# Attention in rounds: two query blocks share a slot between TensorE's main matmuls, and a slot runs transposes, scores, values

## What is computed

```python
# first block: window of 128 keys, per query block the block before and its own
scores = jnp.einsum("bnqhgd,bnkhd->bnhgqk", q, kw) * ATTN_SCALE
scores = jnp.where(mask, scores, -jnp.inf)
probs = softmax(concatenate([scores, sink]))[..., :-1]
out = jnp.einsum("bnhgqk,bnkhd->bnqhgd", probs, vw)
...
# second block, each of two layers: chunk and the eight chunks before it
scores = jnp.einsum("bnqhd,bnkhd->bnhqk", qc, kb) * (dh ** -0.5)
scores = jnp.where(valid, scores + bias, NEG_INF)
out = jnp.einsum("bnhqk,bnkhd->bnqhd", softmax(scores), vb)
```

## Time and profile before

| | |
|---|---|
| median of 3 runs | 1231.44 us (1231.25 to 1232.39) |
| the profiled execution | 1231.82 us |
| its span | 1229.7 us |
| PE busy | 1220.1 us, 99% |
| DVE, ACT, POOL busy | 711.3 us (58%), 535.8 us (44%), 87.2 us (7%) |
| chain that ended last | 95% PE |

### The profile page before, as it was taken

The page is one execution under the profiler, slowest core; times in us unless marked ns, Lnnn a source line. Parts: engine busy times, 40 slices in busy tenths (PEclk is TensorE's granted clock), DMA queues, the critical chain, the costliest instruction groups (busy, mean ns, idle before and its releaser), DMA issues.

```text
span 1229.7 us, 16394 instructions
## 1 busy us (share of the span) xinstructions
PE 1220.1 (99%) x5966; PEld 985.6 (80%) x5966; DVE 711.3 (58%) x1352; ACT 535.8 (44%) x956; POOL 87.2 (7%) x79
## 2 busy tenths in 40 slices
PE   9999999999999999999999999999999999999998
PEld 7888777888888888888888887778888887778886
DVE  5555765464577776775652546654555236564654
ACT  4522553444444344342242414454654325454653
POOL 3000000001100000000010100033002000033000
PEclk9999999999999999999999999999999999999999
DMA  6333222322333223333223521222223431122221
GB/s 210 106 101 103 70 69 69 102 87 87 102 103 102 80 91 102 102 103 102 85 96 103 205 82 58 68 69 69 69 69 111 164 100 55 52 69 69 69 86 69
DMA packets 98203, 114.06 MB, mean 93 GB/s; under 512 B 3801, under 2 KB 82875, under 8 KB 98011
## 3 DMA queue, kind: packets, MB, share of 16 engines
q1 hardware_dynamic: 95755, 107.69, 26.6%
q10 hardware_dynamic: 2384, 5.51, 1.3%
HBM read 111.05 MB, written 2.14 MB: 92 GB/s over the span
## 4 chain that ended last, share of the span: by engine, by line
PE 95%; DVE 1%; ACT 1%; issue 1%; DMA 1%; POOL 0%; SPq 0%; DVEq 0%; ACTq 0%; POOLq 0%
PE main L574 22%; PE main L576 22%; PE main L575 22%; PE aux L664 3%; PE aux L574 3%; PE aux L576 3%; PE aux L575 3%; PE aux L643 3%; PE main L883 2%; PE main L885 2%; PE main L884 2%; PE aux L655 2%; PE main L958 1%; PE main L957 1%; PE main L956 1%
## 5 line engine op out<-in xcount | busy, mean ns | idle before, releaser
L574 PE MATMUL main<-x_hi,w_hi 128*128 128x512 f32 x984 | 393.6, 400 | 0.2 <-DVE w_lo L1459 0.2
L576 PE MATMUL main<-x_hi,w_lo 128*128 128x512 f32 x984 | 383.8, 390 | 0.0
L575 PE MATMUL main<-x_lo,w_hi 128*128 128x512 f32 x984 | 383.7, 390 | 0.0
L1378 DVE TENSOR_TENSOR w_lo<-raw,w_hi 128x1024 fp32r<-128x1024 f32 x192 | 237.9, 1240 | 250.7 <-ACT w_hi L998 246.6
L998 ACT ACTIVATE w_hi<-raw 128x1024 fp32r<-128x1024 f32 x192 | 202.3, 1055 | 260.0 <-PE main L576 156.0
L576 PEld LDWEIGHTS main<-x_hi,w_lo 128*128 128x128 f32 x984 | 184.7, 188 | 40.1
L574 PEld LDWEIGHTS main<-x_hi,w_hi 128*128 128x128 f32 x984 | 184.9, 188 | 38.2 <-issue 2.1
L575 PEld LDWEIGHTS main<-x_lo,w_hi 128*128 128x128 f32 x984 | 185.2, 188 | 35.2
L1036 ACT ACTIVATE soft_pair<-soft_pair,neg_peak 128x256 f32<-128x256 f32 (+3 forms) x64 | 33.6, 526 | 50.4 <-DVE neg_peak L1431 50.4
L1415 DVE TENSOR_TENSOR up_in<-main,factor 128x512 f32<-128x512 f32 x44 | 30.4, 690 | 37.9 <-PE main L576 34.9
L883 PE MATMUL main<-w_hi,x_hi 128*128 128x512 f32 x128 | 50.5, 394 | 0.0
(11 more groups left out here) (264 smaller groups left out, 1837.3 us busy)
## 6 DMA issues: line engine op xcount, KB each, us to landing
raw<-in_w_in_dram SPq DMA_DIRECT2D x98, 512.0 KB, 4.4
raw<-in_w_up_dram SPq DMA_DIRECT2D x44, 512.0 KB, 3.9
raw<-in_w_out_dram SPq DMA_DIRECT2D x24, 512.0 KB, 4.0
raw<-in_w_down_dram SPq DMA_DIRECT2D x22, 512.0 KB, 4.2
rel<-band_rows ACTq DMA_DIRECT2D x2, 2048.0 KB, 9.5
x_rows<-in_x_dram SPq DMA_DIRECT2D x4, 512.0 KB, 8.0
raw<-in_w_attn_branch_dram SPq DMA_DIRECT2D x4, 512.0 KB, 3.4
raw<-in_w_conv_branch_dram SPq DMA_DIRECT2D x4, 512.0 KB, 4.4
```

Of the source, the lines that this page charges most:

```text
L574: pe.matmul(bank, hi, right_hi[j], start=first and j == 0, stop=False)
L575: pe.matmul(bank, hi, right_lo[j], start=False, stop=False)
L576: done = pe.matmul(bank, lo, right_hi[j], start=False, stop=last and j == len(rows) - 1)
L1378: dve.tensor_tensor(w_lo[:, u % 4, :, :], raw_unit(u), w_hi[:, u % 4, :, :].bitcast(F32), ALU.subtract).then_inc(lo_ready, 1)
```

## The change

The two attentions' steps are grouped into rounds, each with up to four key blocks per head (eight rounds in the first block, ten in each layer of the second). A slot now works on rounds: transposes of round r - 2, scores of round r, values of round r - 3, in this order. In the first block there is one slot per unit, after its fourth k-step (11 slots, units 20 to 30); in the second a slot comes every six k-steps, from k-step 92 of the layer (unit 11, after its fourth) on (13 slots, up to unit 20). DVE normalises round r - 1 ahead of softening round r. ACT and DVE place a slot ahead of the unit's own work as before. The transposes use the banks `aux[2]` and `main[3]` in the first block too, so that its units 20 to 30 share three main banks. The tiles for probabilities hold 512 columns per half, two in turn.

```diff
+ROUNDS1 = [[(t, 2 * j), (t, 2 * j + 1)] for t in range(4) for j in range(2)]
+ROUNDS2 = [steps for t in (0, 2) for steps in
+           ([(t, 0), (t, 2)], [(t, 3)], [(t + 1, 0), (t + 1, 2)], [(t, 1), (t + 1, 1)], [(t + 1, 3)])]
+ATT2_SLOTS = [92 + 6 * r for r in range(len(ROUNDS2) + 3)]
...
 def main_bank(u):
+    if ATT1 <= u < ATT1 + len(ROUNDS1) + 3:
+        return (u - ATT1) % 3
...
+        def turn(n, r, spans, soft):
+            if n >= 1:
+                pe.wait_ge(turned_ready, n)
+            for half in range(2):
+                pe.wait_ge(probs_ready, 2 * n + half + 1)
+                for j in range(spans[-1][3].stop // P):
+                    done = pe.transpose(block_of(turned_banks[half], j), block_of(soft(r, half), j), ident[:])
+                done.then_inc(probs_turned, 1)
+        def score(n, spans, queries, keys):
+            for t, b, blocks, columns in spans:
...
                 for half in range(2):
+                    if n >= 1 and columns.start == 0:
+                        pe.wait_ge(peaked, 2 * n - 1 + half)
...
+        def attention_slot(r, first, rounds, queries, keys, value, soft, turned):
+            if 2 <= r < len(rounds) + 2:
+                turn(first + r - 2, r - 2, rounds[r - 2], soft)
+            if r < len(rounds):
+                score(first + r, rounds[r], queries, keys)
+            if 3 <= r < len(rounds) + 3:
+                mix(first + r - 3, rounds[r - 3], value, turned)
...
+                def between(k, i=i):
+                    if 8 * i + k in ATT2_SLOTS:
+                        slot2(ATT2_SLOTS.index(8 * i + k))
...
+        def copy_turned(n, spans, turned):
+            if n >= 1:
+                act.wait_ge(mixed, n)
+            width = spans[-1][3].stop
+            for half in range(2):
+                act.wait_ge(probs_turned, 2 * n + half + 1)
+                done = act.activation(turned[:, half, 0:width], turned_banks[half][:, 0:width], ACT.Copy)
             done.then_inc(turned_ready, 1)
...
+        def attention_slot(r, first, rounds, soft, turned, sinks):
+            if r < len(rounds):
+                exps(first + r, r, rounds[r], soft, sinks)
+            if 2 <= r < len(rounds) + 2:
+                copy_turned(first + r - 2, rounds[r - 2], turned)
...
+        def slot1(r):
+            if 1 <= r < len(rounds1) + 1:
+                normalise(r - 1, r - 1, rounds1[r - 1], soft1, True)
+            if r < len(rounds1):
+                soften(r, r, rounds1[r], lambda t, b, half: window[:, 0 if b else P:256], 0.125,
+                       lambda t, half: sink_cols[:, 2 * t + half:2 * t + half + 1], soft1)
+            if 3 <= r < len(rounds1) + 3:
+                read_mixed(r - 3, mixed_tile(q1, ROUNDS1[r - 3]))
```

More of the change, by code:

```diff
@@ L582, in operands_wait, with project @@
                 pe.wait_ge(bank_empty, emptied(last_use(u)))
-        def project(u, phase, order=tuple(range(KT)), middle=None, hi=x_hi, lo=x_lo, ready=x_ready,
-                    wait=False):
+        def project(u, phase, between=None, hi=x_hi, lo=x_lo, ready=x_ready, wait=False):
             operands_wait(u)
             bank = all_banks[main_bank(u)][:]
-            def tile_wait(j):
+            for k in range(KT):
                 if wait:
[L591 to L598, removed]
+                    pe.wait_ge(ready, KT * phase + k + 1)
+                done = products(u, bank, [k], [hi[:, k, :]], [lo[:, k, :]], k == 0, k == KT - 1)
+                if k == KT - 1:
+                    done.then_inc(unit_done, 1)
+                if between:
+                    between(k + 1)
         def sum_tokens(column, *squared):
@@ L633, in turn_v, with mix @@
             done.then_inc(v_turned, 1)
[L635 to L640, removed]
+        def mix(n, spans, value, turned):
+            pe.wait_ge(turned_ready, n + 1)
+            if n >= 1:
+                pe.wait_ge(mixed_read, n)
+            for step, (t, b, blocks, columns) in enumerate(spans):
+                for j, kb in enumerate(blocks):
+                    for half in range(2):
+                        rows = slice(64 * half, 64 * half + 64)
+                        column = columns.start + j * P
+                        done = pe.matmul(aux[3][rows, step * P:(step + 1) * P], value(t, kb, half),
+                                         turned[:, half, column:column + P],
+                                         start=j == 0, stop=j == len(blocks) - 1)
+            done.then_inc(mixed, 1)
@@ new lines, in turn @@
+        def turn(n, r, spans, soft):
[8 more added lines that the diff above has]
+            for t, b, blocks, columns in spans:
+                query = queries[:, t, b * P:(b + 1) * P]
+                key = keys(t)[:, blocks[0] * P:(blocks[-1] + 1) * P]
@@ L659, in score @@
[L659 to L674, removed]
+                    done = pe.matmul(aux[half][:, columns], query[rows], key[rows], start=True, stop=True)
@@ L1053, in attention_slot @@
-        def attention_slot(s, first, blocks, soft, turned, sink):
-            if s < 16:
-                exps(first + s, blocks(s), soft, sink(s))
-            if 2 <= s < 18:
-                copy_turned(first + s - 2, blocks(s - 2), turned)
+                act.wait_ge(peak_ready, 2 * n + half + 1)
+                for step, (t, b, blocks, columns) in enumerate(spans):
+                    which = (slice(None), n % 2, half, slice(step, step + 1))
+                    if sinks:
+                        act.activation(sink_exp[which], sink_cols[:, 2 * t + half:2 * t + half + 1],
+                                       ACT.Exp, bias=neg_peak[which])
+                    block = soft(r, half)[:, columns]
+                    done = act.activation(block, block, ACT.Exp, bias=neg_peak[which],
+                                          accum_out=total[which])
@@ L1447, in normalise @@
             for half in range(2):
-                block = soft(i, half, n * P)
-                dve.tensor_scalar(block, block, share[:, i % 2, half:half + 1], None, ALU.mult)\
-                    .then_inc(probs_ready, 1)
+                for step, (t, b, blocks, columns) in enumerate(spans):
+                    block = soft(r, half)[:, columns]
+                    done = dve.tensor_scalar(block, block, share[:, n % 2, half, step:step + 1], None, ALU.mult)
+                done.then_inc(probs_ready, 1)
```

259 lines of the change are left out of this document (110 added, 149 removed).

## The result

| | before | after |
|---|---|---|
| time, median of 4 runs (us) | 1231.39 (1231.25 to 1232.39) | 1246.15 (1245.36 to 1246.56) |
| ratio, 95% interval | | 1.0117 (1.0100 to 1.0135) |
| profiled execution, its span (us) | 1231.82, 1229.7 | 1246.28, 1244.4 |

The kernel became **slower by 14.8 us**. The forecast had 4.0, and its range ended at 1240. The direction came out, the size did not. The kernel before, timed again beside each group of experiments, had medians of 1231.38 to 1231.49, so times of different groups can be compared.

A forecast was written before the change was run, and what follows sets the result against it. PE, busy 99% of the span, was taken to bound the kernel: its stream -9.0 us, new waits for ACT's copies +13.0, sum +4.0, so 1235.4 us; range 1228.5 to 1240.

The forecast's parts named there:

- PE's stream, -9.0: PE's work in all attention slots: fewer full slots, 39 to 19, save 9.5 us, less 0.45 at opening and closing slots.
- Entry from transposes 0.09: PE going from transposes into scores, unseen in the trace: assumed 0.09 us, as from a main into scores.
- second pair of scores free: In rounds with two query blocks, 20 second pairs of scores were taken to cost 0, upper bound 4.4 us.
- mains 0.34 apart at the slot's end: Values before a main end the slot: that pair of mains stands 0.34 us apart where 0.23 is usual, 0.11 more.
- That the copies would wait, and the loop behind it: PE's transposes wait for ACT's copies behind a loop over ACT and DVE: waits +13 us in all, 17 of them.
- slot 10, where ACT's two half copies of 0.63 come in too, 7.3 + 1.3 less 7.3, 1.3: Slot 10 of each second attention: PE waits 1.3 us, the loop lengthened by ACT's two half copies.
- the 1.0 that was summed apart for the transposes' entries: Each of the 17 waits ends with 0.06 us that a transpose costs behind another kind: 1.0 us in all.
- The first attention, 4.3: Slots 3 to 8: loop 18.1 us over two rounds against PE's 16.7, so 1.4 us lost three times, 4.3.
- Second pair pays: Rival: every pair of scores pays its own entry on PE, +1.4 to +4.4 us, 1236.8 to 1239.8; chance 0.12.
- late weights: Rival: DVE falls behind, so PE waits some 0.5 us at unit starts in half of 37 slots, 1245; chance 0.05.
- The loop fits: Rival: the loop is no longer than PE's stretch, only the saving is left, 1222.4; chance 0.15.
- 0.15 us for each of 17 waits: Error allowed in each of PE's waits for ACT's copies, beside 1.5 for the saving; the forecast's own range 1232 to 1239.

The follow-up runs named there:

- e7: Changed kernel with the edits of e1, e2 and e3 together, PE's slot order as in the change: 1221.58 us.
- e2: Changed kernel, but DVE softens round r before it normalises round r-1: 1230.80 us.
- e3: Changed kernel, but in a slot ACT copies the transposed probabilities of round r-2 before taking the exponentials of round r: 1222.53 us.
- e1: Changed kernel, but DVE reads a unit's bank into one of two buffers `straight` by turns: 1241.06 us.
- e6: Kernel of e1, with POOL's two passes over a rotary tile cut to 32 of 512 columns: 1237.09 us.
- e5: Changed kernel, but PE transposes the identity 28 times into an unread bank corner before slot 10's transposes in each second attention: 1244.11 us.
- e10: As e5, on the changed kernel, with 19 identity transposes in place of 28: 1242.48 us.
- e9: Changed kernel with the first attention's slots one unit later (ATT1 21 in place of 20): 1243.92 us.

## Why the prediction missed

**PE's stream, -9.0: right.** e7, where no attention waits, is 9.9 us below the kernel before. Entry from transposes 0.09, second pair of scores free, mains 0.34 apart at the slot's end: each as said. In the changed kernel itself the losses of all slots add up to 24.3 us and the span grew by 14.7, which leaves 9.6. (A slot's loss is here the distance of the mains around it, less the same distance in e7.)

**That the copies would wait, and the loop behind it: right.** e2 and e3 change only the order of calls on DVE or on ACT, and give back 15 and 24 us. Outside slot 10 the second block's attentions lost 3.6 and 2.1 us, where 3.2 and 1.8 were summed. Slot by slot it fits as well: in the first layer slots 3, 4, 5, 6 and 9 lost 1.0, 1.2, 0.7, 0.4 and 0.3, against 0.5, 1.4, 0.7, 0.4 and 0.2, and slots 7 and 8 nothing, as forecast.

**The step that failed: "slot 10, where ACT's two half copies of 0.63 come in too, 7.3 + 1.3 less 7.3, 1.3".** It lost 6.4 and 5.8 us (6.2 in the expectations is 0.2 too low). Two terms were missing.

- *POOL's leg.* The half copies were priced as ACT's time alone. They also release POOL, whose two passes (1.78 + 1.29) release DVE's read at L1415, ahead of the weights, the normalising and the softening. PE's wait became 4.0 us, 2.7 more than summed, in each layer: 5.4. With two buffers the wait is 2.6, and with POOL's passes cut it is the forecast 1.3 (e1, e6). The kernel before has that wait of DVE too, but PE waited for nothing there:

```profile
805.14 0.69 DVE L1415 TENSOR_TENSOR straight<-main,factor 128x512 f32<-128x512 f32 x1 [1.54 <-POOL rq L1971]
```

- *The clock.* The forecast let a wait cost its own length. Waits of 4.0 us also brought the granted clock to 0.50, for another 2.3 and 1.6: 3.9 (e5, e10).

Together 9.3 of the 10.8 us that the forecast was short. The rest is made up of 2.1 in the first attention, 0.7 in the other slots of the second block and 0.3 in slot 10, less the 1.0 that was summed apart for the transposes' entries and the 0.6 that the stream saved more than forecast.

**The first attention, 4.3: measured 6.4.** Slots 5 and 6, and slots 7 and 8, lost 1.5 us a pair, where 1.4 was summed; the surplus is all in slots 3 and 4, which lost 3.4. Of it 1.3 were lateness that DVE brought along (e9): its first softening starts at 128.16, behind the convolution, while the loop was summed as if DVE were free. The cause of the other 0.7 is open.

**The rivals.** "Second pair pays" and "late weights" fell with the rows above. "The loop fits" was the wrong rival for the faster side: not a shorter loop but another order takes it off PE's path, and then the time it gave, 1222.4, is near what e3 and e7 measured (1222.53 and 1221.58). Its chances are counted a little apart: 0.14 for faster and 0.02 for same are 0.16, not 0.15, which changes nothing.

**The range** had 0.15 us for each of 17 waits. Errors of that kind did stay small, at most 0.4 us in a slot of the second block outside slot 10. What it lacked was a case in which one slot has another member in its loop, and the price that a long wait has beyond itself.

## What to carry to other kernels

Ask of a copy that a busy engine waits for what stands ahead of it in its queue: here it was the exponentials of a later round, and putting the copies ahead of them was worth 24 us. Follow every release of a step that gets into a loop, through the idle engines too: POOL is busy for 7% of the span and still set the longest wait. And a wait of several microseconds on TensorE is to be priced with its clock: here it added 2.3 and 1.6 us to waits of 4.0, and matmuls whose result nobody reads kept it up.

## What the runs showed beyond that

*Waits of the same length did and did not bring the clock down.* In e2 PE waits 2.33 us in slot 10 of both layers, in one execution. In the first the clock stays at 1.00; in the second it is low from 1083.8 to 1087.2, and the transposes start 0.22 us apart:

```profile
807.99 0.66 PE L667 MATMUL aux<-ident,soft_pair 128*128 128x128 f32 x4 [2.33 <-ACT turned L1053]
1083.81 1.12 PE L667 MATMUL aux<-ident,soft_pair 128*128 128x128 f32 x4 [2.33 <-ACT turned L1053]
```

Slot 10 lost 1.6 us more in the second layer than in the first. Likewise the first attention's first wait, of 2.56 or 2.57 us, had a fall behind it in e1, e6 and e10 and none in the changed kernel and e5. What decides between the two was not found. It may be what moves a kernel's time from run to run: of e1's runs, those at 1239.7 and 1240.2 us have a mean granted clock of 0.997, those at 1241.9 and 1242.8 have 0.996 and 0.994.

*A fall of the clock costs nothing where later waits take it up.* In e10 the clock is low from 149.6 to 153.1, behind the first wait of the first attention. PE's waits there, slots 3 and 6:

```profile
148.19 0.66 PE L667 MATMUL aux<-ident,squares 128*128 128x128 f32 x4 [2.57 <-ACT turned L1057]
175.40 0.55 PE L667 MATMUL aux<-ident,soft_half 128*128 128x128 f32 x3 [0.37 <-ACT turned L1057]
```

Slot 3 lost 1.6 us more there than in the changed kernel, but the slots behind it so much less (the wait of slot 6 is 0.37 us in place of 1.04) that slots 3 to 8 together lost the same: 6.5 us in e10 and 6.4 in the changed kernel. Behind slot 10 no scores follow and no wait is left to take it up, so the fall counts in full.

*DVE and POOL hold each other up, whichever comes second.* In e1 three pairs of instructions met, and each time the later one got longer. The subtraction started at 810.35, while POOL's first pass still ran (to 810.97): 0.5 us longer. POOL's second pass started at 811.05, while the subtraction still ran (to 812.05): 0.9 longer. The normalisings started at 812.17, while that pass still ran (to 813.20): 0.8 longer. The Trainium skill's SBUF — State Buffer, section SBUF: two separate sides, says that DVE instructions with two inputs in SBUF and POOL share a port pair as an exclusive lock, so that the one that comes second fully blocks. The trace agrees for the subtraction and POOL's second pass, each of which was lengthened by most of its overlap with the one before (0.5 of 0.62 us and 0.9 of 1.00). The normalisings have only one tensor as input, and were held up all the same.
